# Summing a conditioning product over partitions: from 128 TensorE transposes and ScalarE sums to 32 transposed VectorE reductions and four TensorE products

## The reference

```python
def trunk_layer(x, xc, c_act, cc_act, w_mod, b_mod, ...):
    mod_x = jnp.split((c_act @ w_mod + b_mod)[:, None, :], 6, axis=-1)
    mod_c = jnp.split(cc_act @ w_mod + b_mod, 6, axis=-1)
    hx = modulate(rms_norm(x, g_pre_mix), mod_x[0], mod_x[1])
    hc = modulate(rms_norm(xc, g_pre_mix), mod_c[0], mod_c[1])
    ...
    x = x + mod_x[2] * rms_norm(y_x, g_post_mix)
    f_x = swiglu(modulate(rms_norm(x, g_pre_ffn), mod_x[3], mod_x[4]), w_ffn_in, w_ffn_out)
    return x + mod_x[5] * rms_norm(f_x, g_post_ffn)
```

## Time and profile before

| | us |
|---|---|
| median of 3 runs (lowest, highest) | 2872.79 (2870.65, 2873.93) |
| the profiled execution | 2874.57 |
| its span, first to last instruction | 2872.7 |
| TensorE busy (matmuls) | 2814.8 |
| VectorE busy | 2125.3 |
| ScalarE busy | 434.2 |
| GpSimd busy | 352.4 |

### The profile page before, as it was taken

How to read it: one execution, slowest core, us unless ns; L and a number is a source line. 1 busy time by engine, 2 the same in 40 slices (tenths; PEclk the granted TensorE clock), 3 DMA queues, 4 the chain that set the end, 5 groups by cost and what they waited for, 6 DMA issues and landing times.

```text
span 2872.7 us, 35402 instructions
## 1 busy us (share of the span) xinstructions
PE 2814.8 (98%) x13380; PEld 2461.9 (86%) x13380; DVE 2125.3 (74%) x3308; ACT 434.2 (15%) x959; POOL 352.4 (12%) x438
## 2 busy tenths in 40 slices
PE   8999999999999999999999999999799999999998
PEld 7888888888888888888887888888688888888887
DVE  5887777988889888888775558787666676555454
ACT  2221112011211112110012122220200000000000
POOL 1012221011121121211110001110011110010000
PEclk9999999999999999999999999999899999999999
DMA  8677666676666666667774455456476776566553
GB/s 264 215 254 222 205 204 203 206 251 214 209 208 211 204 202 206 212 238 241 265 246 144 147 148 146 125 154 222 139 218 212 213 213 204 169 155 204 172 175 123
DMA packets 274986, 571.65 MB, mean 199 GB/s; under 512 B 24522, under 2 KB 25432, under 8 KB 274304
## 3 DMA queue, kind: packets, MB, share of 16 engines
q1 hardware_dynamic: 244112, 460.44, 52.2%
q0 software_dynamic: 30416, 108.87, 12.1%
q10 hardware_dynamic: 288, 0.07, 0.0%
HBM read 565.37 MB, written 3.93 MB: 198 GB/s over the span
## 4 chain that ended last, share of the span: by engine, by line
PE 70%; issue 18%; DVE 6%; DVEq 3%; DMA 1%; POOL 1%; ACT 1%; POOLq 0%; ACTq 0%
PE PS L552 65%; DVEq L980 1%; DVE sums L981 1%; DVE sums L978 1%; DVE sums L983 1%; PE PS L611 1%; DVE mem L1075 1%; PE PS L580 1%; DMA ring<-in_w_in 1%; PE PS L603 1%; DVE ring L979 1%; PE PS L747 0%; PE PS L638 0%; PE PS L663 0%; DVEq L998 0%
## 5 line engine op out<-in xcount | busy, mean ns | idle before, releaser
L552 PE MATMUL PS<-sums,mem 128*128 128x256 f32 x4080 | 1216.5, 380 | 0.0
L552 PE MATMUL PS<-ring,mem 128*128 128x256 f32 x3800 | 1076.0, 380 | 2.1 <-DVE sums L983 2.1
L552 PEld LDWEIGHTS PS<-sums,mem 128*128 128x128 f32 x4080 | 777.4, 191 | 106.5
L552 PE MATMUL PS<-ring,act_t 128*128 128x256 f32 x3112 | 846.8, 381 | 3.9 <-DVE sums L983 3.3
L552 PEld LDWEIGHTS PS<-ring,mem 128*128 128x128 f32 x3800 | 718.9, 191 | 99.7 <-DVE sums L983 3.3
L552 PEld LDWEIGHTS PS<-ring,act_t 128*128 128x128 f32 x3112 | 584.5, 191 | 81.5 <-issue 4.6
L978 DVE TENSOR_TENSOR sums<-ring 128x512 f32<-128x512 f32 x432 | 312.0, 722 | 423.9 <-PE PS L552 386.4
L1075 DVE SCALAR_TENSOR_TENSOR mem<-mem,small 128x512 f32<-128x512 f32 x480 | 352.9, 756 | 33.9 <-DMA mem<-in_w_mod 3.0
L981 DVE TENSOR_TENSOR sums<-sums,ring 128x512 f32<-128x512 f32 x432 | 312.2, 723 | 33.1 <-issue 0.9
L983 DVE TENSOR_TENSOR sums<-sums,ring 128x512 f32<-128x512 f32 x432 | 309.0, 715 | 32.1
L552 PE MATMUL PS<-sums,act_t 128*128 128x256 f32 x1104 | 328.5, 379 | 0.0
(11 more groups left out here) (240 smaller groups left out, 1285.2 us busy)
## 6 DMA issues: line engine op xcount, KB each, us to landing
ring<-in_w_in SPq DMA_DIRECT2D x240, 512.0 KB, 3.7
mem<-in_w_mod POOLq DMA_DIRECT2D x192, 512.0 KB, 5.0
ring<-in_w_up SPq DMA_DIRECT2D x176, 512.0 KB, 3.8
ring<-in_w_ffn_in SPq DMA_DIRECT2D x176, 512.0 KB, 3.7
ring<-in_w_down SPq DMA_DIRECT2D x88, 512.0 KB, 4.6
ring<-in_w_ffn_out SPq DMA_DIRECT2D x88, 512.0 KB, 3.7
ring<-in_w_out SPq DMA_DIRECT2D x64, 512.0 KB, 4.3
ring<-in_w_branch_a SPq DMA_DIRECT2D x16, 512.0 KB, 3.8
```

The lines of the kernel that those rows point to most:

```text
L552: mm = pe.matmul(product(g, j), of(j, 2 * (c if part is None else part) + q), weights(j, n, q), start=lead and j in OPENS, stop=tail, skip ...
```

## The change

The 32 results are no longer summed by TensorE and ScalarE one by one. At the last half of a block VectorE adds up its accumulator in groups of 32 partitions: one reduction for each result, with `apply_transpose`, which turns each 32 by 32 square and sums it to one column, so that [128, 512] becomes [128, 16] in `mod_parts`. Partition 32 q + r of it holds, for quarter q of the partitions, the sums of columns 32 b + r. The four quarters are added by TensorE, for many blocks at once: one product with a 0/1 matrix `fold` (ones where the partitions agree modulo 32), whose moving operand is 16 columns a result. There are four such products, and the table `SUMS` gives each its results, the blocks that have to be done, and its place. VectorE reads the product from bank 7, with the bias added, in four small instructions (`mod_add`). ScalarE no longer takes part, VectorE no longer waits at a block's first half, and bank 7 has four users for the sums instead of 32. `fold` is made once at the start from the identity matrix (one reduction, three copies). `d_t` moves into `mem`, and its memset to the `ctx` stage; GpSimd's load of the level masks waits for `job_acc` instead of a sum.

```diff
-SUMS_AFTER = {}
-_h = 0
...
-            _late = 4 if _n < N0["gate"] else 5 if _n < N0["up"] else 2
...
+SUMS = [(0, 8, 16, N0["down"] + 25), (8, 20, 18, N0["down"] + 35), (20, 28, 20, N0["wout2"] + 13),
+        (28, 32, 24, N0["up2"] + 66)]
...
             def mod_sums(n):
-                for b, v in SUMS_AFTER.get(n, ()):
-                    bank7_take("sum", b, v)
-                    pe.wait_ge(s["job_acc"], b + 1)
-                    which = acc_of(b, v)
-                    for q in range(4):
-                        mm = pe.transpose(PS[:, 7, q * P:(q + 1) * P], acc[:, which, q * P:(q + 1) * P], ident[:])
-                    mm.then_inc(s["bank7_full"], 1)
...
+                bank7_take("sum", b)
+                pe.wait_ge(s["job_acc"], blocks)
+                parts = mod_parts[:, lo % 28:lo % 28 + hi - lo, :].rearrange("p i c -> p (i c)")
+                pe.matmul(PS[:, 7, 0:16 * (hi - lo)], fold[:], parts, start=True, stop=True)\
+                    .then_inc(s["bank7_full"], 1)
...
-                    if part == 0:
-                        for which, _ in vectors:
-                            before = sum_before(b, which)
-                            if before is not None:
-                                ve.wait_ge(s["bank7_full"], bank7_turn("sum", *before) + 1)
-                    else:
-                        ve.drain()
+                    ve.drain()
...
                     if part == 7:
-                        ve.drain().then_inc(s["job_acc"], 1)
...
+                        ve.drain()
+                        for which, at_ in vectors:
+                            to = mod_parts[:, (blk + at_ // 2) % 28]
+                            op = ve.tensor_reduce(to, acc[:, which].rearrange("p (b f) -> p b f", f=32), AX, ADD,
+                                                  apply_transpose=True)
+                        op.then_inc(s["job_acc"], 1)
...
+            def mod_add(b):
...
+                ve.wait_ge(s["bank7_full"], bank7_turn("sum", b) + 1)
+                at_, n = 4 * lo - (32 if lo else 0), 4 * (hi - lo)
+                for j in range(4):
+                    rows = slice(32 * j, 32 * j + 32)
+                    op = ve.tensor_tensor(mod[rows, 4 * lo:4 * hi], PS[rows, 7, j:4 * n:4], b_mod[rows, at_:at_ + n], ADD)
+                op.then_inc(s["bank7_free"], 1)
+                ve.drain()
...
+                    if (g, c) == (3, 3):
+                        mod_add(1)
...
-                        sums_kept(ve, 15, 1)
-                        ve.tensor_tensor(mod[:, 0:32], mod[:, 0:32], b_mod[:, 0:32], ADD)
-                        ve.drain()
+                        mod_add(0)
...
-            def mod_keep(n):
...
-                        op = act.activation(block_, block_, ACT.Identity, accum_out=mod[:, col + q:col + q + 1])
```

More of the change, by code:

```diff
@@ L85 @@
 assert sum(HALVES.values()) == 8 * len(MOD_BLOCKS)
-SUMS_AFTER = {}
-_h = 0
[L89 to L95, removed]
-        else:
-            _late = 4 if _n < N0["gate"] else 5 if _n < N0["up"] else 2
[L98 to L113, removed]
+SUMS = [(0, 8, 16, N0["down"] + 25), (8, 20, 18, N0["down"] + 35), (20, 28, 20, N0["wout2"] + 13),
+        (28, 32, 24, N0["up2"] + 66)]
+SUMS_AFTER = {_n: _b for _b, (_, _, _, _n) in enumerate(SUMS)}
+for _, _, _blocks, _n in SUMS:
+    assert sum(HALVES.get(_k, 0) for _k in range(_n - 1)) >= 8 * _blocks
 BANK7, THROUGH7 = [], []
@@ L140 @@
             BANK7.append(("up_gate", _p // 8, _p % 8 - 5))
-    for _x in SUMS_AFTER.get(_n, ()):
-        BANK7.append(("sum", *_x))
+    if _n in SUMS_AFTER:
+        BANK7.append(("sum", SUMS_AFTER[_n]))
     _p = _n - N0["down"]
@@ L189, in build @@
         ident, ones = sb("ident", P), sb("ones", P)
-        small = sb("small", 896)
+        small = sb("small", 882)
         first_q = sb("first_q", 2, CN // 2)
-        d_t = sb("d_t", T, parts=33)
+        mod_parts, fold = sb("mod_parts", 28, 16), sb("fold", P)
         PS = ctx.enter_context(nc.psum_tensor("PS", [P, 8, 512], F32))
@@ L597, in mod_sums @@
             def mod_sums(n):
-                for b, v in SUMS_AFTER.get(n, ()):
-                    bank7_take("sum", b, v)
-                    pe.wait_ge(s["job_acc"], b + 1)
-                    which = acc_of(b, v)
-                    for q in range(4):
-                        mm = pe.transpose(PS[:, 7, q * P:(q + 1) * P], acc[:, which, q * P:(q + 1) * P], ident[:])
-                    mm.then_inc(s["bank7_full"], 1)
+                if n not in SUMS_AFTER:
+                    return
+                b = SUMS_AFTER[n]
+                lo, hi, blocks, _ = SUMS[b]
+                bank7_take("sum", b)
[3 more added lines that the diff above has]
+                    .then_inc(s["bank7_full"], 1)
             def turn_tokens(key, src, part):
@@ L1078, in mod_halves @@
                     if part == 7:
-                        ve.drain().then_inc(s["job_acc"], 1)
-            def sums_kept(eng, *key):
-                eng.wait_ge(s["bank7_free"], bank7_turn("sum", *key) + 1)
-            ve.memset(d_t[2 * RANK:2 * RANK + 1, :], 1.0)
+                        ve.drain()
[5 more added lines that the diff above has]
+            def mod_add(b):
+                lo, hi, _, _ = SUMS[b]
+                ve.wait_ge(s["bank7_full"], bank7_turn("sum", b) + 1)
[5 more added lines that the diff above has]
+                ve.drain()
+            ve.wait_ge(s["first_loaded"], 32)
+            ve.wait_ge(s["setup_done"], 1)
+            ve.tensor_reduce(fold[:, 0:32], ident[:].rearrange("p (q e) -> p e q", e=32), AX, ADD)
+            ve.drain()
+            for q in range(1, 4):
+                ve.tensor_copy(fold[:, 32 * q:32 * q + 32], fold[:, 0:32])
             norm_combine("mix", 0, ext_x, "forms_mix")
@@ L1544, in _ @@
                     step(n)
+                    if (g, c) == (3, 3):
+                        mod_add(2)
+                        ve.scalar_tensor_tensor(scale_x2, mod[:, 96:112], 1.0, g_pre2, ADD, MUL)\
+                            .then_inc(s["mod_ready"], 1)
                     if (g, c) == (0, 0):
@@ L1585, in _ @@
                     if (i, j) == (9, 1):
-                        sums_kept(ve, 23, 0)
-                        ve.tensor_tensor(mod[:, 112:128], mod[:, 112:128], b_mod[:, 80:96], ADD)
-                        ve.drain()
+                        mod_add(3)
                         ve.wait_ge(s["gate_stored"], 16)
@@ L1634, in norm_keep @@
                 op.then_inc(s["bank7_free"] if key in ("ctx", "ffn") else n["kept"], 1)
-            def mod_keep(n):
-                for b, v in SUMS_AFTER.get(n, ()):
-                    blk, two = MOD_BLOCKS[b]
-                    col = 4 * blk + (0 if two and v == 0 else 32)
-                    act.wait_ge(s["bank7_full"], bank7_turn("sum", b, v) + 1)
-                    for q in range(4):
-                        block_ = PS[:, 7, q * P:(q + 1) * P]
-                        op = act.activation(block_, block_, ACT.Identity, accum_out=mod[:, col + q:col + q + 1])
-                    op.then_inc(s["bank7_free"], 1)
             for dst, src in first:
@@ L1724, in _ @@
                             turn_keep(g - 1, 0)
-                    mod_keep(N0["proj"] + 4 * g + c)
             for u in range(8):
@@ L1843, in _ @@
                         value_base(10, c - 1)
-                    mod_keep(N0["down"] + 11 * g + c)
                     if g == 3 and c >= 3:
@@ L1968, in _ @@
                         open_gate(U_GROUP[1])
-                    mod_keep(N0["wout2"] + 4 * g + c)
                     if g and c == 1:
```

24 lines of the change are left out of this document (7 added, 17 removed).

## The result

| | before | after |
|---|---|---|
| median (lowest, highest), us | 2873.36 (4 runs) | 2852.6 (2852.05, 2853.87; 4 runs) |
| ratio after to before, 95% interval | | 0.993 [0.9912, 0.9947] |
| profiled execution, its span | 2874.57, 2872.7 | 2853.87, 2852.1 |

A forecast was written before the change was run, and what follows sets the result against it. TensorE, busy 98% of the span, was taken as the bound. The terms -14.1 - 6.9 + 1.0 + 0.5 - 1.4 - 2.9 = -23.8 us, put on the median 2872.8, gave 2849.0 us, range 2844 to 2858.

The forecast's parts named there:

- Part 1: All 32 sums: dropping their transposes, 0.44 us each, frees 14.1 us of pure TensorE time.
- Part 2: TensorE's waits around bank 7 in `up`, `branch` and `down` go with the sums: 6.9 us saved.
- The 0.87 of a sum in `up`: First sum of a block waits behind gate transposes for VectorE's side taps; 0.87 us each, five make 4.4.
- both singles: One sum each in `branch` and `down` where ScalarE holds things up, 0.7 and 1.4 us, about 2.5 in all.
- Part 3: Four new products on TensorE cost 0.23, 0.35, 0.23 and at most 0.23: 1.0 us added.
- So it should not wait: Each new product stands behind a chunk starting two or more chunks after the last half it needs; no wait.
- Part 4: 32 new VectorE reductions at 0.69 us each; TensorE delayed only at `wout`, 0.5 us given back.
- The start of `wout`: Block 5's reduction makes VectorE late for line 1208, whose result TensorE transposes; 0.5 us given back.
- 3.3 of 3.8: Per block of `up`: reductions 1.5 plus TensorE 1.8 us earlier use 3.3 of VectorE's 3.8 us of waiting.
- the rival's formula: Dearer reduction, D over 0.69 us: 2 D - 1.0 in five `up` blocks, 2 D in `down`, D at `wout`; chance 0.12.
- Part 5: VectorE's waits at a block's first half go: 1.4 us saved behind `wout`, 2.9 in `down`.
- I count the clock as kept: In `down`, the shorter TensorE wait of 0.9 us brings no half-speed stretch, so the 1.7 us lost is saved.

## Why the prediction was right, point by point

**Part 1, the transposes.** Right, 14.0 for 14.1. The experiment with one transpose of four took away three quarters of it.

**Part 2, the waits in front of the sums.** Right, 7.1 for 6.9. The 0.87 of a sum in `up` were 0.93 and both singles were as read. In the list of waits they are 3.6 + 0.7 + 1.4; that the distance between starts loses more than the idle time was seen in the earlier trace rows and holds.

**Part 3, the new products.** The first three cost what their columns say, 0.22, 0.33 and 0.22. "So it should not wait" failed for the fourth. TensorE in the changed kernel, chunk 66 of `up2`:

```profile
2441.85 0.60 PE L595 MATMUL PS<-ident,mem 128*128 128x128 f32 x4
2443.13 0.43 PE L587 MATMUL PS<-mod_parts,fold 128*128 128x64 f32 x2 [0.68 <-ACT mem L1957]
2443.40 1.08 PE L533 MATMUL PS<-ring,act_t 128*128 128x256 f32 x4
```

The product stands right behind four transposes into the same bank 7, and ScalarE must read those first. 1.28 us pass between the starts where the transposes alone take 0.44. I had looked at who needs the bank after the product and at the half that it needs, but not at who held it ahead of it. Moved by a chunk, the wait is gone. That is 0.9 of the some 3 us that were missing.

**Part 4, the reductions.** The size taken was right, 0.71 for 0.69; it came from the nearest row. The Trainium skill, page "Vector Engine (DVE) Microarchitecture Reference", section "3.8 The reshape front-end and per-opcode configuration", says that the array that turns the squares keeps up one element per cycle and lane, and the trace agrees with 711 ns beside 686. The Trainium skill, page "VectorE: DVE Perf Modes", section "Why `tensor_reduce` can't reduce along partition axis", says that the lanes have no path across; this does not hold for groups of 32 partitions, for 32 such reductions ran, at 4% over a plain one. What was mis-sized is the effect. The start of `wout` gave back 0.9 and not 0.5:

```profile
578.67 0.63 PE L667 MATMUL PS<-ident,mem 128*128 128x128 f32 x4 [0.46 <-DVE mem L1204]
```

0.65 are in front of these transposes, as the idle time says with its late pickup, and 0.24 more at the next two weight sums, which stand behind the same late VectorE. `up` shows 0.5 in four spots, at nothing in the sum. "3.3 of 3.8" was right as a sum of durations, but the 3.8 are not free where they are needed: the experiment with two reductions puts the margin at 0.5 us a block, and with three almost nothing of the addition is covered (7.5 of 8). So the rival's formula was too kind, and the sign turns at about 2.3 us of reducing for a result (three reductions and two drains), not at 2.7.

**Part 5, VectorE's waits at a first half.** Behind `wout` 1.6 for 1.4, and the experiment that puts the wait back shows its cause. In `down` 2.45 for 2.9 in the first pair of executions, but by luck, as the repeats show. TensorE in the changed kernel:

```profile
1317.80 1.13 PE L533 MATMUL PS<-ring,mem 128*128 128x256 f32 x4 [1.35 <-DVE sums L967]
```

The wait is 1.35 and not 0.9. VectorE no longer waits at the first half, as forecast (the 3.62 of the earlier trace rows are gone):

```profile
1302.24 1.23 DVE L1277 TENSOR_TENSOR x_tok<-x_tok,mem 128x1024 f32<-128x1024 f32 x1
1303.56 0.88 DVE L1051 TENSOR_SCALAR mem<-mem,small 128x512 f32<-128x512 f32 x2
```

But VectorE's work ahead of it begins with a landing of weights. In the changed kernel, and then in the kernel before:

```profile
1272.34 0.69 DVE L962 TENSOR_TENSOR sums<-ring 128x512 f32<-128x512 f32 x1 [4.90 <-DMA ring<-in_w_down]
```

```profile
1286.25 0.69 DVE L978 TENSOR_TENSOR sums<-ring 128x512 f32<-128x512 f32 x1 [4.31 <-DMA ring<-in_w_down]
```

Counted from the first product of `down`, this landing lets VectorE go on after 47.58 us in the changed kernel, and after 48.09, 48.49 and 48.52 in its repeats. TensorE's later wait is 1.35, 1.85, 2.23 and 2.28: each tenth that the weights come later stands in the wait. (In the kernel before it did not: the landing at 48.40 went with the shortest of its four waits, 1.89, since VectorE waited for a sum behind it anyway.) My step took VectorE to be free to come earlier by its own saved wait; it did not say that a load, which does not come earlier with TensorE (47.35 before), opens its work there. By these four executions the term was worth far less than the 2.45 of the first. TensorE's wait is 1.9 on average where it was 2.1 before, so about 0.2 of the 1.2 us forecast for its shortening are there. Less the lost clock, `down` takes 277.5 to 277.9 before and 272.5 to 273.4 after, and all but 0.2 us of that difference belongs to the other parts (sums, new products, the wait ahead of `ctx`). With the double half moved away from there, the wait is gone though the landing is as late (1272.48, 48.28 after the first product).

"I count the clock as kept" came true in three of four executions of the changed kernel, but in one of four of the kernel before as well. So of the 2.9 forecast here 1.7 were a matter of chance on both sides.

**What was not in the sum.** `ctx` and `mix` came out 1.6 us longer in this pair of executions. I had put them at zero. But for the 0.26 at the last wait of `mix` nothing shows that the change does anything there; the repeats show that the place of the half-clock stretches, and whether a wait hides one, moves them by that much and more.

The sum again, from the forecast: -23.8, and to it +0.9 (the bank ahead of the fourth product), +0.4 (`wout`), +0.5 (`up`), +0.45 (`down`), -0.2 (waits of part 2), -0.2 (behind `wout`), +1.6 (`ctx` and `mix`), -0.4 (starts, which differ between executions of one kernel by as much and more) = -20.8, for the -20.6 measured. It closes for this pair of executions; in `down` and in `ctx` with `mix` luck stands on both sides of it, 1.7 us in its favour and 1.6 against.

## What to carry over

Where a bounding engine shares a bank, look at each new user from both sides: who needs the bank after it, and who still holds it ahead of it. Reserve time of an engine that comes second counts only between the work and its deadline; a sum of its waits over a block overstates it, here 1.0 for 0.5 us, and doubling the added work measures it directly. And before a microsecond is put down to a change, look in more than one execution of both kernels at the time that the granted clock took in that stage, and at whether a wait behind it gave it back.

## What the runs showed of the hardware

- VectorE's reduction with turned 32 by 32 squares, [128, 512] to [128, 16] in float32, takes 711 ns, next to 686 for a plain one over as many elements.
- An idle time of TensorE of about 2 us in `down` is followed by a stretch at 1.2 instead of 2.4 GHz in some executions and not in others of the same program. It fell behind 1.89, 2.12 and 2.21 us of idle time and not behind 2.08 in the kernel before; behind 2.23 and not behind 1.35, 1.85 and 2.28 in the changed one. In the experiments it fell behind 2.51 (one transpose of four) and not behind 2.41 (reductions twice and three times).
- What a half-clock stretch takes, a later wait can give back: the same 16.66 us in `mix` hold 1.57 us less of waiting where such a stretch lies in them.
- In `ctx` and `mix` the clock falls to half speed also while TensorE is recorded as fully busy (1640 to 1650 us: 10.00 of 10.00 busy, 0.69). In all 14 profiled executions each such fall begins 2.9 to 4.4 us behind the start of the eight products of line 740 (756 before), which fill 33 of 128 rows and take 3.7 us at full clock; two executions have none. Whether these products bring it on was not tried.
